# Experts with 64 slots of their own, router logits taken inside the output projection, final norm by slot

## The reference, cut to what matters

```python
x = x + mixed @ w_o                       # 2048 x 2048
h = rmsnorm(x, norm2_g)
g_logits = h @ wg + bg                    # 4 groups, the best one is taken
sub      = h @ ws + bs                    # 4 experts in each group, the best two of the chosen group
e_w      = softmax(two values) * p_group
for e in range(16):
    gate, up = split(h @ wu[e])           # 2048 x 1024, that is 8 MB
    out += combine[:, e] * ((silu(gate) * up) @ wd[e])   # 512 x 2048, that is 4 MB
y = rmsnorm(x + out, final_norm_g)
```

## Time and profile before

| | |
|---|---|
| median of 3 runs | 1927.06 us (1924.11 to 1928.66) |
| the profiled execution, its own time | 1928.34 us |
| its span from first to last instruction | 1926.6 us |
| TensorE busy | 1796.4 us (93%) |
| VectorE busy | 1202.6 us (62%) |
| ScalarE busy | 1015.8 us (53%) |
| GpSimd busy | 119.9 us (6%) |
| read from HBM | 386.15 MB |

### The profile page before, as it was taken

One profiled execution on the slowest core, in us unless ns is written; L12 is line 12 of the kernel. 1 busy time (PEld: TensorE's weight loads), 2 busy tenths in 40 slices (PEclk: granted clock), 3 DMA queues, 4 the chain that ended last, 5 costly groups with the idle time before them and its releaser, 6 DMA issues.

```text
span 1926.6 us, 30826 instructions
## 1 busy us (share of the span) xinstructions
PE 1796.4 (93%) x11292; PEld 1562.2 (81%) x11292; DVE 1202.6 (62%) x1444; ACT 1015.8 (53%) x1318; POOL 119.9 (6%) x156
## 2 busy tenths in 40 slices
PE   5999989999999999999999999679989999999995
PEld 5999989999899888898999999557656766666763
DVE  5898864444444444444444444369868978887985
ACT  6666753333444444433333433458747766765773
POOL 2554510000000000000000000000000000000000
PEclk9999989999999999998999999789989999999997
DMA  7565655567645566544655777149949967995992
GB/s 188 151 174 142 170 133 159 158 172 192 175 134 136 152 165 164 142 114 124 171 158 158 197 191 193 48 172 371 375 176 375 372 253 296 379 345 208 371 362 67
DMA packets 418413, 394.12 MB, mean 205 GB/s; under 512 B 18624, under 2 KB 376336, under 8 KB 409104
## 3 DMA queue, kind: packets, MB, share of 16 engines
q1 hardware_dynamic: 407472, 385.40, 63.7%
q10 hardware_dynamic: 10432, 4.79, 1.0%
q0 software_dynamic: 448, 3.15, 0.7%
HBM read 386.15 MB, written 7.14 MB: 204 GB/s over the span
## 4 chain that ended last, share of the span: by engine, by line
PE 80%; DVE 8%; issue 5%; ACT 5%; DMA 1%; POOL 0%; SPq 0%; ACTq 0%; DVEq 0%; POOLq 0%
PE bank L885 15%; PE bank L886 15%; PE bank L887 15%; PE bank L1061 10%; PE bank L1065 9%; PE bank L1063 9%; ACT wH L572 2%; PE bank L1088 1%; DVE sL L1448 1%; PE bank L955 1%; DVE x L1461 1%; ACT L632 1%; DVE rc L1238 1%; DVE xn L1178 1%; PE bank L988 1%
## 5 line engine op out<-in xcount | busy, mean ns | idle before, releaser
L572 ACT ACTIVATE wH<-ring 128x1024 fp32r<-128x1024 f32 x320 | 336.0, 1058 | 551.9 <-PE bank L887 544.9
L885 PE MATMUL bank<-hH,wH 128*128 128x288 f32 x2048 | 614.2, 300 | 10.6 <-DVE hL L1350 4.9
L1165 DVE TENSOR_TENSOR wL<-ring,wH 128x1024 fp32r<-128x1024 f32 x320 | 387.9, 1230 | 378.4 <-ACT wH L572 365.2
L886 PE MATMUL bank<-hL,wH 128*128 128x288 f32 x2048 | 607.1, 296 | 0.0
L887 PE MATMUL bank<-hH,wL 128*128 128x288 f32 x2048 | 606.7, 296 | 0.0
L1448 DVE TENSOR_TENSOR sL<-raw,sH 128x1024 fp32r<-128x1024 f32 x384 | 467.0, 1224 | 88.4 <-ACT sH L794 78.4
L794 ACT ACTIVATE sH<-raw 128x1024 fp32r<-128x1024 f32 x384 | 404.0, 1060 | 127.0 <-PE bank L1065 126.9
L885 PEld LDWEIGHTS bank<-hH,wH 128*128 128x128 f32 x2048 | 388.4, 190 | 18.0 <-issue 12.1
L886 PEld LDWEIGHTS bank<-hL,wH 128*128 128x128 f32 x2048 | 388.2, 190 | 0.4
L887 PEld LDWEIGHTS bank<-hH,wL 128*128 128x128 f32 x2048 | 387.9, 189 | 0.0
L1061 PE MATMUL bank<-sH,hgH 128*96 128x512 f32 x512 | 164.9, 404 | 0.3
(11 more groups left out here) (249 smaller groups left out, 1643.5 us busy)
## 6 DMA issues: line engine op xcount, KB each, us to landing
raw<-in_expert_w_up SPq DMA_DIRECT2D x128, 1024.0 KB, 5.1
ring<-in_w_in SPq DMA_DIRECT2D x112, 1024.0 KB, 7.0
raw<-in_expert_w_down SPq DMA_DIRECT2D x64, 1024.0 KB, 5.0
ring<-in_w_pb SPq DMA_DIRECT2D x16, 1024.0 KB, 8.9
ring<-in_w_pa SPq DMA_DIRECT2D x16, 1024.0 KB, 9.0
ring<-in_w_o SPq DMA_DIRECT2D x16, 1024.0 KB, 5.9
cK<-in_cache_k SPq DMA_DIRECT2D x16, 256.0 KB, 2.8
cV<-in_cache_v SPq DMA_DIRECT2D x16, 256.0 KB, 3.3
```

The lines of the kernel that those rows point to most:

```text
L572: a.activation(wH[2 * (slot % 2) + half][:, :, :], ring[slot][:, 8 * half:8 * half + 8, :], ACT.Copy).then_inc(hi_ready, 1)
L885: pe.matmul(dst, hi, rH[:, k, :], start=(k == 0), stop=False)
L886: pe.matmul(dst, hi, rL[:, k, :], start=False, stop=False)
L1165: v.tensor_tensor(lo[:, :, :], ring[slot][:, 8 * half:8 * half + 8, :], hi[:, :, :].bitcast(F32), ALU.subtract).then_inc(lo_ready, 1)
```

## The change

1. **Up products on 64 slots of each expert.** Within its group each expert gets a list of its own with at most ES = 64 rows. The stationary operand of an up product is 128 columns wide: 64 columns H and 64 columns L of the same rows side by side (`hgs`). So `up_half` does 4 products of 512 columns where `three` did 6; the H part and the L part of the result lie in different partitions and are added afterwards (`gl`, two ScalarE copies and two VectorE additions). The rows reach these slots by `gather` and `spread` products, 12 rounds for a group, interleaved with the down products of the group before. `remap` brings an expert's activations back to the 96 slots of its group.
2. **Down products** stay at 96 slots, 6 for a half, except an expert's last piece (`WHOLE`), which is not split: 4 full-precision products with the unsplit `atF`. So 22 halves for each expert are split instead of 24. The norm's gain is no longer applied to the rows but to the up weights, as the scale of the split.
3. **No gap between groups.** The pieces of all 16 experts form one list (`STREAM`), in which the first four up pieces of the next expert stand ahead of an expert's down pieces. The buffers `raw` are five instead of six.
4. **W_o and router.** In each W_o tile TensorE also adds the residual rows (6 small products with an identity) and takes the logits of the tile before (2 products of 288 columns). Squares are summed tile by tile. The norm passes, the 48 turns and the 16 logit products after W_o are gone. The 7 small transfers of the router's weights stand before the tiles of `w_pa` in SyncE's queue, and the residual rows are fetched at the end of attention.
5. **End.** The residual stays in slot order and is added in PSUM (`residual`). After a group ScalarE squares its 96 rows, VectorE scales them, and GpSimd stores them by two indirect DMAs, one for each output.

When a group has over 96 rows or an expert over 64, further passes run; the data here needs none.

```diff
-RAW = 6
+RAW = 5
+LEAD = 4
+STREAM = []
+for _e in range(NE):
+    STREAM += [(_e, s) for s in range(LEAD if _e else 0, PU)]
+    if _e + 1 < NE:
+        STREAM += [(_e + 1, s) for s in range(LEAD)]
+    STREAM += [(_e, PU + m) for m in range(PD)]
+GL_AT = [NTH[GATED[e]] + 3 for e in range(NE - 1)] + [LAST]
+SILU_AT = [NTH[GATED[e]] + 4 for e in range(NE - 1)] + [LAST + 1]
+ACT_AT = [NTH[GATED[e]] + 6 for e in range(NE - 1)] + [LAST + 2]
+AT_AT = [NTH[TURN_AT[e]] + 3 for e in range(NE - 1)] + [LAST + 3]
+ROUND_AT = [None] * 8 + [2, 5, 8, 11]
+for _g in range(NG - 1):
+    for _j in (1, 2, 3):
+        ROUND_AT += [DOWN_AT[EPG * _g + _j] + 3 * r for r in range(4)]
...
# SyncE: a buffer is free when its piece is split, or, for WHOLE, when TensorE has used it
+                elif n >= RAW:
+                    old = n - RAW
+                    if STREAM[old][1] == WHOLE:
+                        sp.wait_ge(eh_done, 2 * old + 2)
+                    else:
+                        sp.wait_ge(sL_ready, NTH[2 * old + 1] + 1)
+                fetch(n % RAW, ds(e, 1), s)
...
# TensorE, W_o tile m
+                    if m > 0 and k == 12:
+                        y_turn(m - 1)
+                        logits(m - 1)
...
+                pe.wait_ge(xL_ready, m // 4 + 1)
+                for f in range(FT):
+                    for x in (x1H, x1L):
+                        ins = pe.matmul(acc[b][:, f * TB:(f + 1) * TB], x[:, f, m * P:(m + 1) * P],
+                                        identR[0:TB, 0:TB], start=False, stop=(x is x1L), skip_group_check=True)
...
+            def up_half(banks, w, hi, lo, k):
+                for c in range(2):
+                    pe.matmul(banks[c][:, :], w, hi[:, c * 512:(c + 1) * 512], start=(k == 0), stop=False)
+                for c in range(2):
+                    ins = pe.matmul(banks[c][:, :], w, lo[:, c * 512:(c + 1) * 512], start=False,
+                                    stop=(k == KT - 1))
+                ins.then_inc(eh_done, 1)
...
+            def spread(dst, k, e, n):
+                for h, x in enumerate((xsH, xsL)):
+                    ins = pe.matmul(dst[:, :, h, :], x[:, k * P:(k + 1) * P], R[:, e:e + n, 0, :],
+                                    start=True, stop=True)
+                return ins
...
+                if t == DOWN_AT[e]:
+                    pe.wait_ge(atL_ready, e + 1)
+                    if j == 0:
+                        need(pe, yo_ready, 4 * g)
+                        residual(xsH, True, False)
+                        residual(xsL, False, False)
...
+                if s == WHOLE:
+                    if half == 0:
+                        pe.wait_ge(raw_in[n % RAW], 16 * (n // RAW + 1))
+                    for c in range(2):
+                        nb = 2 * half + c
+                        ins = pe.matmul(out4[nb][0:CAP, :], atF[:, :],
+                                        raw[n % RAW][:, nb * 512:(nb + 1) * 512], start=False,
+                                        stop=(j == EPG - 1), skip_group_check=True)
+                    ins.then_inc(eh_done, 1)
...
# VectorE
+                if s < PU:
+                    v.scalar_tensor_tensor(sL[buf][:, :], src, g2[:, 2 * s + half:2 * s + half + 1],
+                                           sH[buf][:, :].bitcast(F32), ALU.mult, ALU.subtract).then_inc(sL_ready, 1)
...
+                    if i == GL_AT[e]:
+                        v.wait_ge(gl_ready, 2 * e + 1)
+                        v.tensor_tensor(gl[:, 0:FF], pair[e % 2][0][0:ES, :], gl[:, 0:FF], ALU.add)\
+                         .then_inc(gate_ready, 1)
+                        v.wait_ge(gl_ready, 2 * e + 2)
+                        v.tensor_tensor(gl[:, FF:], pair[e % 2][1][0:ES, :], gl[:, FF:], ALU.add).then_inc(up_s, 1)
...
# GpSimd
+            for g in range(NG):
+                pool.wait_ge(idx_ready, g + 1)
+                pool.wait_ge(yo_ready, 4 * (g + 1))
+                rows_out(g)
```

More of the change, by code:

```diff
@@ L231, in build @@
+    raw_xr = [sb(f"raw{s}", [P, 2048]) for s in range(2, RAW)]
+    R = sb("R", [CAP, EPG, 2, ES], F32R)
+    G = sb("G", [TB, FT, CAP], F32R)
     assert here[0] <= at_mixed
[L232 to L241, removed]
@@ L250, in build @@
-    pos = sb("pos", [TB, FT, NG + 1])
+    picks = sb("picks", [TB, FT, 20])
+    rank = sb("rank", [TB, FT, NE])
+    cnt = sb("cnt", [P, 20])
     cmax = sb("cmax", [P, 1])
[L252 to L255, removed]
+    assert here[0] <= at_ring
+    here[0] = at_ring
+    sH = [sb(f"sH{s}", [P, 1024], F32R) for s in range(HALVES)]
+    sL = [sb(f"sL{s}", [P, 1024], F32R) for s in range(HALVES)]
+    xsH = sb("xsH", [CAP, D], F32R)
@@ L500, in _ @@
+                first = 0
+                for width in WINDOWS:
+                    again(first, width)
+                    first += NG * width
+                sp.wait_ge(eh_done, HALF_N + 24 * EPG * NG * sum(WINDOWS))
         @block.gpsimd
@@ L751, in _ @@
                  .then_inc(mixsplit_s, 1)
-            def wo(i, last=False):
-                for j in range(4):
-                    m = 4 * i + j
-                    if not (last and j >= 2):
-                        ahead(T_WO, 4, i, j)
-                    a.wait_ge(half_done, 2 * (T_WO + m + 1))
-                    a.activation(yT[:, j % 2, :], acc[j % 2][:, 0:T], ACT.Copy).then_inc(yT_ready, 1)
-                    a.wait_ge(yT_ready, m + 1)
-                    a.sem_inc(acc_used[j % 2], 1)
@@ new lines, in _ @@
+            part(0)
+            for m in range(KT):
+                if m + 2 < KT:
+                    split(T_WO + m + 2, (m + 2) % RING)
+                else:
+                    expert_split(2 * (m + 2 - KT))
+                    expert_split(2 * (m + 2 - KT) + 1)
+                if m in (1, 2, 3):
+                    part(m)
+                if m > 0:
+                    x1_lo(m - 1)
+                v.wait_ge(yT_ready, m + 1)
+                v.wait_ge(x1TH_ready, m + 1)
+                v.tensor_tensor(x1TL[:, m % 2, :], acc[m % 2][:, 0:T], x1TH[:, m % 2, :].bitcast(F32),
+                                ALU.subtract).then_inc(x1TL_ready, 1)
@@ L1503, in groups @@
-            def groups(c):
-                assign(0, c)
-                group(0, c, first=(c == 0))
-                with v.Fori(1, NG) as g:
-                    group(g, c)
-            v.wait_ge(consts2, 5)
-            v.wait_ge(routed, 1)
-            n = v.value_load(cnt_i[0:1, 0:1], min_val=0, max_val=T)
-            groups(0)
-            with v.If(n > CAP):
-                for c in range(1, CHUNKS):
-                    groups(c)
-                v.wait_ge(added, 4 * FT * (NG * CHUNKS - 1))
```

1162 lines of the change are left out of this document (760 added, 402 removed).

## The result

The changed kernel takes **1896.66 us** (median of 4 runs, 1895.62 to 1898.73) against 1927.72 us before (4 runs). The ratio is 0.9844, 95% interval 0.9827 to 0.9861: 1.6% faster, where 4.6% was forecast, and outside the range. The profiled span is 1894.4 us.

| stage | before | forecast | after |
|---|---|---|---|
| to the end of W_o | 1218.0 | 1232.6 | 1231.4 |
| router | 58.0 | 26.6 | 31.9 |
| experts | 622.1 | 563.5 | 616.5 |
| end | 28.5 | 14.7 | 14.6 |

A forecast was written before the change was run, and what follows sets the result against it. TensorE was taken to set the pace inside groups, with 19.2 us gaps between them. W_o's end 1232.6, router 26.6, experts 563.5 and end 14.7 summed to a span of 1837.4, forecast 1838 us, 4.6% less, range 1790 to 1885.

The forecast's parts named there:

- W_o: W_o tiles: added logit and small products cost 12.2 us, late residual copies 2.4; W_o ends at 1232.6.
- Router: From W_o's end to the first expert product: 26.6 us against 58.0, range 23 to 34.
- End: After the last expert product: 14.7 us against 28.5, with 7 for issue and landing of both stores.
- An expert, in order: Expert stage: 16 cycles of 32.1 make 514, plus 51 on top; 565 in full, 555 taken, 563.5 with the last expert.
- The border: Between groups: slots and rows 1.5 us, VectorE's final scaling 3.5, residual products 1.85; squares cost nothing after the first three groups.
- The plain cycle: One expert between unsplit pieces: 20.1 us through up halves and activation, then 12.0 of TensorE's down products, 32.1 in all.
- Rounds: Gathers and spreads inside the expert stage, for three groups: three of four gather rounds 4.2 us, spreads 5.3.
- (a): Rival, expert stage: the transfers bind and all else hides, 510 us there, 1792 in all; chance 0.12.
- (b): Rival, expert stage: the transfers bind at a lower rate, 546 to 597 us there, 1829 to 1880; chance 0.13.
- (c): Rival: TensorE's clock goes to 1.2 GHz in all up stretches, 141 us more, 1979, slower than before; chance 0.05.
- (d): Rival: an uncounted wait in each expert, say behind ScalarE's round copies; 3 us in each of 16, 1886; chance 0.10.
- (e): Rival: groups still stand apart, rounds, slots or residual products waiting at each border; 14 us more, 1852; chance 0.12.

The follow-up runs named there:

- e1: The changed kernel without the final norm's squares and roots for groups 0 to 2, whose results are only multiplied by the gain: 1874.62 us.
- s_norm_spread: The changed kernel with the norm of groups 0 to 2 taken apart, one square and one product between any two splits: 1883.87 us.
- no_root: The changed kernel with the norm's root replaced by a copy that needs no table: 1893.48 us.
- e6: The changed kernel with the norm's gain left out of the up splits on both engines: 1883.69 us.
- w4: The changed kernel with each expert's unsplit down piece, but the last's, four pieces later, behind the next expert's last up piece: 1857.08 us.
- e9: The changed kernel with the norm's steps three places later in both queues and the rounds two halves apart instead of three: 1892.74 us.
- e7: The changed kernel with every transfer of expert weights but the first five bringing half its bytes: 1897.19 us.
- s1_timed: The changed kernel, norm taken apart, unsplit piece four pieces later, one at group borders: 1848.74 us, ratio 0.9591 to the kernel before.

## Why the prediction was wrong

**W_o**: 1231.4 for 1232.6, in part by luck. The logits were taken inside the tiles, as written. From its first product the stage grew by 15.6 us (from 1109.1 to 1218.0 before, 1106.9 to 1231.4 after), where I had 14.6. Within that the small products cost 0.11 each instead of 0.083, and the 2.4 us for late residual copies do not show: TensorE has no wait in the tiles. The rest is a start 2.2 us earlier, which I had not forecast and which varies that much between runs.

**Router**: the way was right, and 31.9 for 26.6 comes mostly from three terms that were mis-sized. Picks came after 9 us and the 24 gathers took 7.6, both as written. The ranks took 3.4 instead of 1.7, the spreads 5.5 instead of 4.0, since half of them ran at the clock's lower level (0.21 instead of 0.11 each), and from there to the first expert product 3.5 passed instead of 1.5:

```profile
1240.32 0.51 PE L1286 MATMUL bank<-picks,before 96*96 96x20 f32 x2 [5.84 <-DVE picks L1813]
...
1254.33 0.30 PE L1346 MATMUL bank<-R,xsH 96*128 96x128 f32 x1 [1.39 <-issue]
...
1256.35 0.42 PE L1346 MATMUL bank<-R,xsH 96*128 96x128 f32 x1
```

**End**: 14.6 for 14.7. The two indirect stores were issued in 0.91 us each, the second at 1888.94, and the span ended 5.5 after that. I took 7 for both; they took 6.7.

```profile
1887.72 0.91 POOL L646 DMA_INDIRECT out<-yo,idx  x1 [128.96 <-DVE yo L1886]
1888.94 0.91 POOL L646 DMA_INDIRECT out<-yo,idx  x1 [0.30 <-issue]
```

**Experts** is the step that failed, "An expert, in order": 563.5 forecast, 616.5 measured. Its plain cycle, VectorE's stretch and then TensorE's, was near (32.89 for 32.1); what it adds at a border, the discount it takes and its count of the rounds were wrong. The 53 us are:

- **The border, 19.3 us.** Its surplus over a plain cycle was 13.8, 13.9 and 12.2 us; I had 6.85 each (slots, scaling, residual products). The prediction counted VectorE's scaling and called the norm free "where the next group's down products come 12 us later". It asked who waits for the result and not what is queued behind its first step: ScalarE's squares wait for the unsplit piece's end, ahead of the split and of the drain that TensorE's next round needs. e1 puts 7.9 us on it and leaves a border of 38.8 for my 38.95, so the norm alone covers the excess. Order makes up to 3.6 of that (s_norm_spread), the root's table loads 0.7 to 1.9 (no_root, measured in the old order, so not to be added up). The rest, with the share of the clock, was not taken apart and stays open. Of the terms I had, the 1.5 us for slots and rows stand in the first expert and the first two borders; the third has none, and is 1.7 us shorter.
- **Leaning below the sum, 10 us.** I took 555 where the terms added up to 565, because buffers might hide some of it. The cycles added up, and more; nothing was hidden.
- **The plain cycle, 11.1 us**: 32.89 instead of 32.1, 14 times. VectorE's split with gain cost 1.28 (back to back every 1.20) where I had 1.17. e6 fits the picture of turns; w4 took only 0.5 to 0.7 us off the plain cycle where the picture gave 1.4 to 2.4, so it is borne out in part.
- **Rounds, 6.2 us**: 11.6 a group instead of 9.5. I counted three of every four. Eleven of a group's twelve rounds lie in its three cycles, and their products come to 11.7 us (4 gather rounds at 1.39, 7 spread rounds at 0.88); the fourth round behind the unsplit piece costs about as much as one inside the down stretch, which e9 shows. The twelfth lies in the border.
- **First and last expert, 6.9 us.** From the first product to the first unsplit piece it took 46.9 us. ScalarE works there with three splits and two copies in turn and nearly no gap, but TensorE is as full (8.00 of 8 us), so the rows don't settle which of them bound, nor how the 6.9 us divide between the two ends:

```profile
1268.89 3.23 ACT L876 ACTIVATE sH<-raw,prm 128x1024 fp32r<-128x1024 f32 x3
1272.03 1.06 ACT L931 ACTIVATE hgs<-bank 128x512 fp32r<-128x512 f32 x2
1272.98 3.22 ACT L876 ACTIVATE sH<-raw,prm 128x1024 fp32r<-128x1024 f32 x3
...
1269.00:1277.00 8.00, 8.00 (x43) 6.60 (x43) 6.71 (x7) 8.00 (x10) 0.00 (x0) 1.00 0.79 269
```

These make 53.5 with their rounding.

**The rivals.** (a) and (b), the transfers: false, e7 changed no cycle but the third border. The read rate did stay near 370 in the expert stage, the prediction's sign of being wrong by the transfers, without their being the cause. (c), the clock: false in the up stretches, where it stayed at 1.00, and true in a small place that I had not named, behind the border's waits. The Trainium skill (TensorE: Matmul & The Clock Gate, HAM oscillation) describes a kernel whose clock fell in each wait for a DMA between its groups of products. The border's rows, with waits of another kind (3.65 us, then 0.84 over 20 us), agree with it. The prediction cited it for short pauses; those stand under the page's next heading (A second HAM failure mode: psum-queue depth-cycling), and the up stretches, which have them (TensorE busy 33.3 of 36 us), kept 1.00. (d), an uncounted wait: its size (48 us in all) was near by luck, its place wrong: ScalarE's round copies cost nothing in nine cycles and 2.9 us at a border. (e), the border: nearest in place. Its 14 us cover rounds and border together, for which 25.5 were measured, and it names the rounds, slots and residual products, not the norm, which made the largest part.

## What to carry to other kernels

When a step is moved into a pipelined stretch, walk each queue that it enters: what its first instruction waits for, and what stands behind it, count as well as when its result is due. A long piece that needs no buffers of the others is worth trying where its engine would wait anyway; that alone gave more than the whole change (40 us against 31), though not by the cycles that the theory named. Add up the terms of a serial chain and don't take a discount for overlap that no row shows; and price an engine's copies by what waits for them, since 4 us of them a cycle turned out to be free.

## What the runs showed of the hardware

- A DMA share of 0.98 at 394 GB/s did not mean that transfers bound: with half the bytes the cycle was 32.88 for 32.89. s1_timed held 401 GB/s over 57 us; whether it was bound by them was not tried:

```profile
1755.00:1812.00 57.00, 53.08 (x206) 34.26 (x205) 52.44 (x48) 45.38 (x49) 0.00 (x0) 1.00 1.00 401
```

The Trainium skill (DMA: Bandwidth & Descriptors, Where 436 GB/s comes from) gives a core about 358 GB/s from HBM; these rows are above that.

- The clock stayed at 1.00 with TensorE busy 33.3 of 36 us in short waits, and fell behind a wait of 3.65 us. A wait that long is not needed: in s_norm_spread it fell to 0.56 with none over 1.85 us. In w4_whole_later it was 0.59 over 20 us with TensorE shown busy 17.59 of them, at the slower pace.
- With a scale for each partition ScalarE's copy of 1024 columns took 1.142 us instead of 1.057, and VectorE's fused product and difference takes 1.280 where the plain difference takes 1.219 (groups by line and form, expert stage):

```profile
L1738 DVE SCALAR_TENSOR_TENSOR sL<-raw,prm,sH 128x1024 fp32r<-128x1024 f32 x252 | 312.7, 1280 | 108.8 <-ACT sH L876 107.2
L876 ACT ACTIVATE sH<-raw,prm 128x1024 fp32r<-128x1024 f32 x252 | 276.5, 1142 | 68.2 <-PE bank L1312 48.0 <-DMA raw<-in_expert_w_up 11.9 <-PE bank L1303 7.9
L1741 DVE TENSOR_TENSOR sL<-raw,sH 128x1024 fp32r<-128x1024 f32 x96 | 114.3, 1219 | 14.0 <-ACT sH L876 12.7
L876 ACT ACTIVATE sH<-raw 128x1024 fp32r<-128x1024 f32 x96 | 100.6, 1057 | 29.3 <-PE bank L1303 27.0 <-PE bank L1312 0.8
```
